# Two ffn stages in which seven block products replace eight: another order of the products, three of four weight sums on GpSimd, the chunk splits named by hand

## The reference

```python
for l in range(DEPTH):
    ...  # three mixers, a gated merge, x = x + merged @ w_o[l]
    h = rms_norm(x, g_ffn[l])
    x = x + (jax.nn.silu(h @ w1[l]) * (h @ w3[l])) @ w2[l]
```

## Time and profile before

| | |
|---|---|
| median of 3 runs | 3365.53 us (3363.88 to 3374.15) |
| profiled execution | 3368.76 us, its span 3367.1 us, mean granted clock 0.98 |
| PE busy | 3254.4 us (97%), 16588 matmuls |
| DVE, ACT, POOL busy | 1988.7 us (59%), 1390.1 us (41%), 673.8 us (20%) |
| DMA | 295.78 MB, mean 88 GB/s |

### The profile page before, as it was taken

How to read it: one execution, slowest core, us unless ns; L and a number is a source line. 1 busy time by engine, 2 the same in 40 slices (tenths; PEclk the granted TensorE clock), 3 DMA queues, 4 the chain that set the end, 5 groups by cost and what they waited for, 6 DMA issues and landing times. The chain is left out here.

```text
span 3367.1 us, 41173 instructions
## 1 busy us (share of the span) xinstructions
PE 3254.4 (97%) x16588; PEld 2770.9 (82%) x16588; DVE 1988.7 (59%) x3012; ACT 1390.1 (41%) x2143; POOL 673.8 (20%) x530
## 2 busy tenths in 40 slices
PE   9999999898899999999898899999999999999998
PEld 7888888788888888887788888888888888888887
DVE  6764865745657755856646555554644357974433
ACT  5643643423336634633423333332332237853321
POOL 1421330111103321420101111111211013431101
PEclk9999999999899999999998899999999999999999
DMA  3122323222232122322222232222223222223232
GB/s 132 55 73 73 105 93 100 79 90 75 70 111 63 64 69 85 104 94 95 75 93 75 66 109 79 85 91 88 82 100 100 95 94 88 94 88 106 90 103 84
DMA packets 85149, 295.78 MB, mean 88 GB/s; under 512 B 9568, under 2 KB 12128, under 8 KB 84960
## 3 DMA queue, kind: packets, MB, share of 16 engines
q1 hardware_dynamic: 84384, 292.76, 26.4%
q10 hardware_dynamic: 576, 0.40, 0.0%
HBM read 291.02 MB, written 2.10 MB: 87 GB/s over the span
## 5 line engine op out<-in xcount | busy, mean ns | idle before, releaser
L675 DVE TENSOR_TENSOR wl<-s_raw,wh 128x1024 fp32r<-128x1024 f32 (+1 forms) x563 | 684.5, 1219 | 618.6 <-ACT wh L616 617.3
L358 PE MATMUL bank<-zh,wh 128*128 128x512 f32 (+1 forms) x2588 | 959.0, 371 | 23.2 <-ACT wh L616 9.0
L358 PE MATMUL bank<-zh,wl 128*128 128x512 f32 (+1 forms) x2588 | 952.1, 368 | 1.9 <-DVE wl L675 1.9
L358 PE MATMUL bank<-zl,wh 128*128 128x512 f32 (+1 forms) x2588 | 951.2, 368 | 2.2 <-DVE zl L678 2.1
L616 ACT ACTIVATE wh<-s_raw 128x1024 fp32r<-128x1024 f32 (+1 forms) x563 | 572.1, 1027 | 500.7 <-PE bank L358 422.4
L358 PEld LDWEIGHTS bank<-zh,wh 128*128 128x128 f32 x2588 | 502.2, 194 | 99.0 <-ACT wh L616 9.9
L358 PEld LDWEIGHTS bank<-zh,wl 128*128 128x128 f32 x2588 | 499.9, 193 | 86.0 <-DVE wl L675 8.7
L358 PEld LDWEIGHTS bank<-zl,wh 128*128 128x128 f32 x2588 | 501.2, 194 | 76.5 <-DVE zl L678 4.0
L733 POOL TENSOR_TENSOR f_t<-f_t 128x512 f32<-128x512 f32 x84 | 114.0, 1357 | 515.4 <-DVE f_t L671 515.4
L739 POOL TENSOR_TENSOR small<-small 128x1 f32<-128x1 f32 (+3 forms) x35 | 43.0, 1228 | 823.7 <-DVE small L668 823.7
L358 PE MATMUL bank<-n_h,wh 128*128 128x256 f32 (+1 forms) x448 | 145.3, 324 | 51.8 <-ACT wh L616 51.8
(11 more groups left out here) (379 smaller groups left out, 5768.5 us busy)
## 6 DMA issues: line engine op xcount, KB each, us to landing
s_raw<-in_wts SPq DMA_DIRECT2D x529, 512.0 KB, 3.4
c_nb<-in_c_bias SPq DMA_DIRECT2D x16, 384.0 KB, 3.3
x<-in_xT SPq DMA_DIRECT2D x8, 256.0 KB, 6.2
out<-x SPq DMA_DIRECT2D x13, 128.0 KB, 1.8
b_mask<-in_b_mask SPq DMA_DIRECT2D x2, 576.0 KB, 4.0
r_d<-in_decay SPq DMA_DIRECT2D x4, 256.0 KB, 3.2
s_raw<-in_wts SPq DMA_DIRECT2D x2, 256.0 KB, 3.6
m_t<-in_mla_tab SPq DMA_DIRECT2D x2, 256.0 KB, 4.8
```

Of the source, the lines that this page charges most:

```text
L358: return self.e.matmul(out, l, r, start=start, stop=stop, skip_group_check=inside)
L675: return self.e.tensor_tensor(out, src, b32(hi), ALU.subtract)
```

## The change

**Order of the products.** TensorE now runs unit i from begin to end: part 0 is now s_b (P7, P5), part 1 is s_raw with the third sum (P1, P6), part 2 the 512 columns as loaded (P2), part 3 the one with the fourth sum (Q4, P3). ScalarE also copies P7 out (c1), so that Q4 can add to the bank; VectorE's v, s2, u7, u6, g2 take the place of s2, s3, u7, g2, u6. P2 waits for ScalarE's s1, Q4 for c1, P3 for v.

**The sums.** `Dve.sums` goes. GpSimd's `gpsimd_sums` makes s_b and the third sum one unit ahead, each unit's before the product f_t of the unit before last. The fourth sum moves from GpSimd to VectorE, behind the wl of part 2.

**The splits.** In S units the chunks are split at points named by hand (`upto`), and no longer by `ahead()` at the end.

**The units 0 to 5.** The normed activations, the token differences n_ta and n_tb and their splits move: n_ta and n_tb from behind unit 1's gate to behind unit 3's, three of the four zh/zl to unit 4 and the last to unit 5. Before, all four stood together ahead of unit 4.

```diff
@@ class Act, high_s
         if part == 0:
-            self.wait_ge("wl", "S2", *unit)
+            self.wait_ge("pl", "S1", *unit)
+            self.cp(wh, m.s_b).then_inc(*self.tell("wh", c))
+        elif part == 1:
+            self.wait_ge("pl", "S2", *unit)
             self.cp(wh, src[:, 0:1024]).then_inc(*self.tell("wh", c))
...
+        else:
+            self.wait_ge("wl", "S4", *unit)
+            self.cp(wh, src[:, 1024:2048]).then_inc(*self.tell("wh", c))
@@ class Dve
-    def sums(self, unit, a, b):
...
-        self.tt(m.s_b, src[:, 0:1024], src[:, 512:1536], ALU.add).then_inc(*self.tell("wl", "S1", *unit))
-        self.wait_ge("wl", "S1", *unit)
-        self.tt(src[:, 512:1024], m.s_b[:, 512:1024], src[:, 0:512], ALU.add).then_inc(*self.tell("wl", "S2", *unit))
...
+        elif part == 2:
+            self.lo(wl[:, 0:512], src[:, 1536:2048], wh[:, 0:512]).then_inc(*self.tell("wl", c))
+            self.wait_ge("wl", c)
+            self.wait_ge("pl", "S2", *unit)
+            self.tt(src[:, 1536:2048], src[:, 512:1024], src[:, 1536:2048], ALU.add).then_inc(
+                *self.tell("wl", ("S4",) + unit, ("rel", a)))
+        else:
             self.lo(wl, src[:, 1024:2048], wh).then_inc(*self.tell("wl", (c,), ("rel", b)))
@@ tensor_unit
     w = L.s_chunk(0, unit, loads)
+    c = L.claim(C, "ev", "u6", *unit)[:, 0:256]
+    L.product(w, 0, token_sum(L, F, 2), 0, c, True, "P7", *unit)
+    d = L.claim(D, "ev", "g2", *unit)[:, 0:256]
+    L.product(w, 1, token_sum(L, F, 0), 0, d, True, "P5", *unit)
+    w = L.s_chunk(1, unit, loads)
     a = L.claim(A, "cp", "g1", *unit)[:, 0:256]
     L.product(w, 0, normed_quarter(L, F, 0), 0, a, True, "P1", *unit)
     b = L.claim(B, "ev", "s2", *unit)[:, 0:256]
     L.product(w, 1, token_sum(L, F, 1), 0, b, True, "P6", *unit)
-    tail()
     w = L.s_chunk(2, unit, loads)
...
     L.wait_ge("cp", "s1", *unit)
     L.product(w, 0, normed_quarter(L, F, 0), 4, a, False, "P2", *unit)
+    w = L.s_chunk(3, unit, loads)
+    L.wait_ge("cp", "c1", *unit)
+    L.product(w, 0, token_sum(L, F, 3), 0, c, False, "Q4", *unit)
+    L.wait_ge("ev", "v", *unit)
+    L.product(w, 1, normed_quarter(L, F, 1), 4, d, False, "P3", *unit)
@@ the new functions of GpSimd
+def gpsimd_sums(L, F, i):
...
+    landed(L, a)
+    landed(L, b)
+    before = F + (i - 1,) if KINDS[i - 1] == "S" else ("f", 0, FF - 1) if F[1] else None
+    if before:
+        L.wait_ge("wl", book.s_at(0, before))
+        L.wait_ge("pl", "S2", *before)
+    L.tt(L.m.s_b, src[:, 0:1024], src[:, 512:1536], ALU.add).then_inc(*L.tell("pl", "S1", *unit))
+    L.wait_ge("pl", "S1", *unit)
+    L.tt(src[:, 512:1024], L.m.s_b[:, 512:1024], src[:, 0:512], ALU.add).then_inc(*L.tell("pl", "S2", *unit))
...
+    gpsimd_sums(L, F, units[0])
+    for i in units:
+        if i + 1 in units:
+            gpsimd_sums(L, F, i + 1)
+        if i - 1 in units:
+            gpsimd_unit(L, F, i - 1)
+    gpsimd_unit(L, F, units[-1])
@@ the new orders of ScalarE and VectorE in a unit
+def scalar_unit(L, F, l, i):
...
+    upto(L, c + 2)
+    if prev and KINDS[prev] == "S":
+        scalar_unit_gate(L, F, prev)
+    scalar_c1(L, F, i)
+    upto(L, c + 3)
+    scalar_s1(L, F, i)
+    if prev:
+        scalar_half_mid(L, F, l, prev)
+    upto(L, c + 4)
+    upto(L, c + 5)
+    scalar_g1(L, F, i)
```

More of the change, by code:

```diff
@@ L73, in __init__ @@
         self.plan, self.turns, self.mark = [], {}, {}
-        self.ring, self.loads = [], []
+        self.ring, self.loads, self.s_chunks = [], [], {}
     def s_at(self, part, unit):
[L78 to L83, removed]
+        return self.s_chunks.get((part, unit), 0)
     def needs(self, c):
         c = min(c, len(self.ring) - 1)
-        after = self.s_next(c)
-        return max([r[-1] for r in self.ring[max(0, c - 8):c + 1]] + ([after[-1]] if after else []))
+        return max(r[-1] for r in self.ring[max(0, c - 8):c + 1])
 class Dry:
@@ L401, in s_chunk @@
         self.book.ring.append(("s", part, unit, *loads))
+        self.book.s_chunks[part, unit] = self.chunk
         c, s = self.chunk, self.chunk % RING
@@ L2547, in vector_token_sum, with was, scalar_c1 @@
         L.tt(by_tile(tb), by_tile(ta), quarter(xb, 0), ALU.subtract).then_inc(*L.tell("ev", "t", *F, 3))
-T_ORDER = (0, 1, 2, 3)
 def s_of(m, i):
     return m.s_s[i % 2]
+def was(i):
+    return KINDS[i - 2]
+def scalar_c1(L, F, i):
+    m = L.m
+    L.wait_ge("mm", "P7", *F, i)
+    if was(i) == "S":
+        L.wait_ge("ev", "v", *F, i - 2)
+    L.cp(s_of(m, i)[0], m.bank[unit_banks(i)[2]][:, 0:256]).then_inc(*L.tell("cp", "c1", *F, i))
 def scalar_s1(L, F, i):
@@ L2707, in vector_units, with upto @@
-def vector_units(L, F, units):
-    for i in (*units, None):
-        prev = units[-1] if i is None else i - 1
-        first = i == units[0] and i == HALF
-        if i is not None and KINDS[i] == "S":
-            vector_s2(L, F, i)
-        if not first and KINDS[prev] == "S":
-            vector_unit_out(L, F, prev)
-            vector_unit_gate(L, F, prev)
-        if i is not None and KINDS[i] == "S":
-            vector_s3(L, F, i)
-        if not first:
-            vector_half_mid(L, F, prev)
-        if i is not None and KINDS[i] == "N":
-            vector_unit_gate(L, F, i)
-        L.ahead()
+def upto(L, c):
+    L.weights(c - L.lead)
@@ L2725, in scalar_ffn1 @@
+def scalar_units(L, F, l, units):
+    for i in units:
+        scalar_unit(L, F, l, i)
+    scalar_unit_gate(L, F, units[-1])
+    scalar_half_mid(L, F, l, units[-1])
+def vector_units(L, F, units):
+    for i in units:
+        vector_unit(L, F, i)
+    vector_g2(L, F, units[-1])
+    vector_unit_gate(L, F, units[-1])
+    vector_half_mid(L, F, units[-1])
+FIRST_S = KINDS.index("S")
+TOKEN_SUMS = {4: (0, 1, 2), 5: (3,)}
 def scalar_ffn1(L, l):
     m, nxt, F = L.m, after_ffn1(l), ("f", l)
-    first = KINDS.index("N")
@@ L2728, in scalar_ffn1 @@
     scalar_rows(L, ("ffn", l))
     L.lead = 2
[L2730 removed]
+    for i in range(FIRST_S):
         if i:
             scalar_half_mid(L, F, l, i - 1)
[L2733 to L2735 removed]
+        for j in TOKEN_SUMS.get(i, ()):
+            scalar_token_sum(L, F, j)
+            L.ahead()
+        if KINDS[i] == "N":
+            scalar_unit_gate(L, F, i)
+        else:
+            scalar_mid_gate(L, F, i)
         if i < 2:
[L2737 removed]
+            scalar_normed(L, F, range(4 * i, 4 * i + 4))
@@ L2738, in scalar_ffn1 @@
         L.ahead()
-    for j in T_ORDER:
-        scalar_token_sum(L, F, j)
-        L.ahead()
-    scalar_units(L, F, l, range(first, HALF))
+    scalar_units(L, F, l, range(FIRST_S, HALF))
     scalar_units(L, F, l, range(HALF, FF))
```

212 lines of the change are left out of this document (87 added, 125 removed).

## The result

The changed kernel takes 3258.3 us (median of 4 runs, 3255.7 to 3261.1) against 3369.8 (3363.9 to 3374.2) of the kernel before in the same comparison: a ratio of 0.967, with a 95% interval of 0.9649 to 0.9692. Its profiled execution took 3259.6 us, span 3257.9, 109.2 less than the span before.

A forecast was written before the change was run, and what follows sets the result against it. A closed wait loop across VectorE, ScalarE, GpSimd and the load, 14.6 us per S unit, was taken as the bound. 3368.8 - 94 (S stretches) - 8 (ffn1 starts) = 3266.8 us profiled, 3263 as median; range 3228 to 3305.

The forecast's parts named there:

- The old loop and its end: S units of ffn1: a closed wait loop through VectorE, ScalarE, GpSimd and load, 14.6 us a unit, which the new order opens.
- The pair and the timetable: S units: GpSimd ops and VectorE ops with two SBUF inputs exclude each other; their locked ops in order give 11.3 us.
- two waits forecast for TensorE: In each S unit TensorE, needing 10.1 us, waits at P2 for s1 and at chunk 3 for the wl of 7.60.
- the load's 11.1: S units: the load released at 7.60 lets the next s_b start at 11.1 us, just inside the period of 11.3.
- s_b at 2.30: GpSimd's add of 1024 columns in S units, taken as twice the held 1.15 us; bounds 2.07 and 2.58.
- The added 0.2 us a unit: S units: allowance for semaphores and clock on top of the 11.3 us period, giving 11.5.
- my 358: The four S stretches after the change: 4 x 20.5 + 24 x 11.5 = 358 us, against 452.3 before.
- 20.5 together: First and last S unit of each half, lacking a product or sums beside them: about 10.4 and 10.1 us.
- The clock: Rival, S units: short stalls still lower TensorE's clock, so it needs 11.9 to 13.1 us; 3294 at 12.8; chance 0.15.
- TensorE as the bound: Rival, S units: GpSimd's sums slip into VectorE's gaps, period 10.1 to 11, 3229 us at 10.1; chance 0.12.
- GpSimd's starvation: Rival, S units: gapless VectorE runs delay each GpSimd op by 2.0 us, period 17.3, time 3402 us; chance 0.05.
- The start of ffn1: Before the S units: a 4.5 us stall goes, 6.4 gained, about 2.4 returns; 4 us saved per layer, 8 in all.

The follow-up runs named there:

- the probes: Two runs on the kernel with all S-unit elementwise work on VectorE (3235.5 us), adding one unneeded GpSimd op a unit: two inputs 3260.7 us, one input 3244.4.

## Why the prediction was right

**The old loop and its end.** Right as far as the runs reach. The new orders, with each sum on the engine of before, give the whole gain (3257.9), so it was the order, and not VectorE's or GpSimd's share of the sums, that cost 14.6 us a unit; that it worked through h_h and the two wh behind it is read from the trace of before, where TensorE waited 23.3 us of a second half for those wh and their wl, and these waits are gone. Three things changed together in the order: TensorE's order of the products (with the copy c1), the places of the splits and the start of ffn1. No run takes the first two apart, so which of them opened the loop isn't shown.

**The pair and the timetable.** Right, and to about 0.1 us in each step; one of the two waits forecast for TensorE, that for the wl of chunk 3, came only in three units of layer 1. The rule of the Trainium skill (SBUF — State Buffer, section "SBUF: two separate sides") that one engine fully blocks the other for a whole instruction agrees with the trace and the probes: wl 2.20 instead of 1.22 beside an op of 1.29. The period is 11.2 us, the pair's; six load slots change nothing in layer 0, so the load's 11.1 is close but not the bound. Only in layer 1 did late loads cost 2.4 us, which the six slots took away.

**s_b at 2.30.** Right where it counts: 2.26 and 2.27 from the moment when it gets the pair; its shortest row, from issue, is 2.40 (2398 ns). The estimate by the 1.96 of the Trainium skill (GPSIMD Engine Reference, section 3.1) was that 2.40; it is the length of an unheld op, and a queued one costs the others less.

**The added 0.2 us a unit** was the term that was too large: it measured nothing, for the timetable came out without it and the clock was 1.00. With the 0.1 by which 11.3 was above 11.2, 24 x 0.3 = 7 of the 10.5 us by which the S stretches are shorter than my 358. The other 3 are in the first and last units of the halves, which I had at 20.5 together: 52.55 - 3 x 11.2 = 19.0 in the first one.

**The clock** as a rival is refuted: waits of 0.4 to 1.3 us, 7.9 us in the 120.1 of layer 0's second half, leave it at 1.00 in all four stretches, where before 25 us of waits in 155.6, single ones up to 3.3 us, stood beside 0.88. I had priced stalls of 1.2 us with the fall that belonged to those. It isn't the length of the longest wait alone, though. Before, the clock fell at 842.5 also after two short waits with only two matmuls between them:

```profile
839.95 0.38 PE L358 MATMUL bank<-n_h,wh 128*128 128x256 f32 x1 [0.77 <-ACT wh L616]
841.21 0.39 PE L358 MATMUL bank<-n_h,wl 128*128 128x256 f32 x1 [0.76 <-DVE wl L675]
842.60:845.80 3.20, 3.20 (x17) 3.20 (x16) 2.69 (x3) 0.89 (x2) 0.00 (x0) 0.50 0.34 110
```

**TensorE as the bound** didn't come with this change, but with all work on VectorE it nearly does (10.33). **GpSimd's starvation** didn't come either: its product took 1.27 to 1.30 us in 30 of 32 units and 2.26 and 2.27 in the other two. In the unit shown it starts at 808.99, where VectorE works from a bank.

**The start of ffn1** is the step that failed. I gave each layer 4 us, with 6.4 gained at unit 4 and 2.4 coming back at unit 5. The wait of 4.5 us (it stood ahead of unit 3) is gone as said, and in layer 0 unit 4 begins 27.0 us behind rrow instead of 34.3, 7.3 earlier. But at unit 5, where 2.5 us of waits stood before, layer 0 lost it all (5.3 + 1.6 us of waits), 0.4 us worse than before; layer 1, with 4.1 us of waits there, kept 5.0; the sum is 4.6 instead of 8. One of the forecast's signs of being wrong, a start of ffn1 as long as before, thus came true in layer 0. I had listed zh and the token differences ahead of unit 5's chunks and left out that GpSimd's first sums, freed from VectorE's order, would run there and hold the pair; the profile of the run that delays them shows 3.1 us for it in layer 0.

Together: forecast 94 + 8, measured 104.8 + 4.6 (and 0.8 late at rrow of layer 0, from outside the stages that change): 3266.8 forecast for the profiled execution, 3259.6 measured. The two misses have opposite signs, so part of the closeness of the total is luck.

## What to carry to other kernels

First find the loop of waits and ask which instruction in it is only there because of its place in an engine's order: the new orders were worth 111 us here, and the moves between engines that came with them nothing in sum. An idle GpSimd is not free for elementwise work: add up what both engines hold the shared pair, since an op of 1.29 us there costs a full VectorE 0.9 to 1.0 us even when nobody needs its result (25.2 by 28, and the held wl), while the same op on VectorE costs 0.6 (798.84 to 799.45, the start of the next). And when work moves to an engine with nothing before it in its order, look at how early it can start, and what it will hold up there.

## What the hardware showed beyond that

- GpSimd's op of 128x512 with two inputs takes 1.29 us, with one input and two constants 0.62, and both exclude VectorE's ops with two SBUF inputs for their whole length (wl of 1.22 held to 2.20 and 1.52).
- An instruction that was held ends sooner after its release than its length alone: wl 1.07 to 1.08 after GpSimd's end, against 1.22 (1.14 from start to start).
- Single TensorE waits of 0.9 to 1.2 us every 11.2 us left the granted clock at 1.00. In the wait of 5.3 us at the start of ffn1, which began at 625.9, it fell to 0.50 at 629.7, and it rose at 639.9, 10.2 us later.
